# Two-layer hybrid decoder on one core: the first K group of the first turn, 256 rows, becomes two of 128 rows, with two blocks held in PSUM and a shorter filler

## The reference

```python
mod = jax.nn.silu(c) @ w_ada + b_ada                 # w_ada: 2048 x 6144
shift, scale, gate = jnp.split(mod, 3, axis=-1)
h = _rmsnorm(x, norm_pre) * (1.0 + scale[:, None, :]) + shift[:, None, :]
z = h @ w_in                                         # w_in: 2048 x 14336
gb, gcin, u, g_c, q, k, v, g_r = jnp.split(z, offs, axis=-1)
y_conv = gb * _causal_short_conv(gcin * u, conv_w) * jax.nn.silu(g_c)
ret = _head_groupnorm(_retention_chunkwise(rope(q), rope(k) * RET_DK ** -0.5, v), gn_gain)
y_ret = ret * jax.nn.silu(g_r)
o = jnp.concatenate([y_conv, y_ret], axis=-1) @ w_out
x = x + gate[:, None, :] * _rmsnorm(o, norm_post)
```

## Time and profile before

| what | value |
|---|---|
| median of 3 runs | 1704.76 us (1704.67 to 1704.78) |
| the profiled execution, its own time | 1705.27 us |
| its span, first to last instruction | 1703.5 us |
| PE busy | 1675.5 us (98%) |
| DVE busy | 1168.8 us (69%) |
| ACT busy | 733.5 us (43%) |
| DMA | 429.25 MB, mean 252 GB/s |

### The profile page before, as it was taken

One profiled execution on the slowest core, in us unless ns is written; L12 is line 12 of the kernel. 1 busy time (PEld: TensorE's weight loads), 2 busy tenths in 40 slices (PEclk: granted clock), 3 DMA queues, 4 the chain that ended last, 5 costly groups with the idle time before them and its releaser, 6 DMA issues.

```text
span 1703.5 us, 19027 instructions
## 1 busy us (share of the span) xinstructions
PE 1675.5 (98%) x7707; PEld 1371.7 (81%) x7707; DVE 1168.8 (69%) x1325; ACT 733.5 (43%) x817; POOL 52.2 (3%) x94
## 2 busy tenths in 40 slices
PE   5999999999999999999999999999999999999998
PEld 4677788888888888888878888888888888888886
DVE  2578768788678778788886455555645555578777
ACT  4454444534444444344464434344344444444442
POOL 4000000000000000000000000000000000000000
PEclk9999999999999999999999999999999999999999
DMA  9999765897798789888865675557556756678884
GB/s 340 383 373 346 229 213 179 290 303 275 242 310 282 251 301 305 307 281 286 292 199 198 198 219 189 186 197 222 180 185 204 222 185 188 209 261 301 286 288 178
DMA packets 233655, 429.25 MB, mean 252 GB/s; under 512 B 8664, under 2 KB 50024, under 8 KB 232800
## 3 DMA queue, kind: packets, MB, share of 16 engines
q1 hardware_dynamic: 225888, 408.97, 70.3%
q10 hardware_dynamic: 7680, 19.07, 4.2%
HBM read 417.57 MB, written 2.10 MB: 246 GB/s over the span
## 4 chain that ended last, share of the span: by engine, by line
PE 97%; DVE 1%; DMA 1%; SPq 0%; issue 0%; ACT 0%; POOL 0%; DVEq 0%; ACTq 0%
PE Z L1398 31%; PE Z L1400 30%; PE Z L1399 30%; PE A L1437 1%; DMA front_last_stage<-in_w_ada 1%; PE A L1486 1%; PE B L1486 0%; SPq L601 0%; PE A L1450 0%; PE A L1579 0%; PE B L1593 0%; PE B L1591 0%; PE B L1592 0%; PE Z L1445 0%; DVE xt L1029 0%; PE A L1580 0%
## 5 line engine op out<-in xcount | busy, mean ns | idle before, releaser
L649 ACT CAST w_hi<-stage 128x1024 fp32r<-128x1024 f32 x574 | 602.5, 1052 | 921.4 <-PE Z L1400 840.0
L885 DVE TENSOR_TENSOR w_lo<-stage,w_hi 128x1024 fp32r<-128x1024 f32 x574 | 696.6, 1222 | 434.5 <-ACT w_hi L649 430.4
L1398 PE MATMUL Z<-w_hi,H 128*128 128x512 f32 x1784 | 702.8, 394 | 0.6 <-DVE part L1135 0.5
L1400 PE MATMUL Z<-w_hi,H 128*128 128x512 f32 x1784 | 695.2, 390 | 0.0
L1399 PE MATMUL Z<-w_lo,H 128*128 128x512 f32 x1784 | 694.7, 389 | 0.0
L1398 PEld LDWEIGHTS Z<-w_hi,H 128*128 128x128 f32 x1784 | 335.0, 188 | 77.9 <-issue 8.4
L1400 PEld LDWEIGHTS Z<-w_hi,H 128*128 128x128 f32 x1784 | 334.9, 188 | 70.6
L1399 PEld LDWEIGHTS Z<-w_lo,H 128*128 128x128 f32 x1784 | 335.2, 188 | 67.7
L906 DVE SCALAR_TENSOR_TENSOR acc<-stage,c_silu,acc 128x512 f32<-128x512 f32 x240 | 180.2, 751 | 6.8
L1398 PE MATMUL Z<-w_hi,YC 128*128 128x512 f32 x256 | 100.2, 391 | 0.0
L1398 PE MATMUL Z<-w_hi,YR 128*128 128x512 f32 x256 | 100.0, 391 | 0.0
(11 more groups left out here) (178 smaller groups left out, 742.7 us busy)
## 6 DMA issues: line engine op xcount, KB each, us to landing
stage<-in_w_in SPq DMA_DIRECT2D x186, 1024.0 KB, 5.2
stage<-in_w_ada SPq DMA_DIRECT2D x64, 1024.0 KB, 5.3
stage<-in_w_out SPq DMA_DIRECT2D x64, 1024.0 KB, 5.3
stage<-in_w_in SPq DMA_DIRECT2D x74, 512.0 KB, 4.8
front_stage<-in_w_ada SPq DMA_DIRECT2D x24, 1024.0 KB, 10.8
front_last_stage<-in_w_ada SPq DMA_DIRECT2D x8, 1024.0 KB, 13.2
behind<-R ACTq DMA_DIRECT2D x14, 448.0 KB, 3.5
taps<-in_conv_w ACTq DMA_DIRECT2D x18, 256.0 KB, 6.4
```

The lines of the kernel that those rows point to most:

```text
L649: N.copy(w_bufs(n, h)[0], stage[:, slot_of(n), 2 * h:2 * h + 2, :]).then_inc(s_hi, 1)
L885: V.tensor_tensor(lo, stage[:, slot_of(n), 2 * h:2 * h + 2, :], hi.bitcast(F32), ALU.subtract)\
L1398: T.matmul(z[:, i, :], hh, wh, start=ch.first and a == 0, stop=False)
L1400: ins = T.matmul(z[:, i, :], hl, wh, start=False, stop=stop)
```

## The change

The first group is split: `FRONT_GROUPS` now begins with two groups of one tile (128 rows) and has six groups. Chunks 0 to 6 are the new group 0, 7 to 13 the new group 1, 14 to 20 the new group 2 (tiles 2 and 3, which were group 1), the early chunks 21 to 23, and everything from there on stands 7 places later. The blocks GG and GB of group 0 stay in their accumulators, and group 1 begins with these two and adds to them; the other five blocks are added on DVE. A piece of w_ada of the first two groups is 16 times 128 rows of 128 columns, where it was 8 times 128 rows of 256 columns (both 1 MiB). The filler is 5 products instead of 8. All tables of the front are new.

```diff
-FRONT_GROUPS = ((0, 2), (2, 2), (4, 4), (8, 4), (12, 4))
+FRONT_GROUPS = ((0, 1), (1, 1), (2, 2), (4, 4), (8, 4), (12, 4))
-EARLY, EARLY_AFTER = (QK, VV, GR), 1
+EARLY, EARLY_AFTER = (QK, VV, GR), 2
+HELD = (GG, GB)
...
-        for b in range(BLOCKS):
-            table.append(Chunk(False, 0, 0, b, g, q, True, True, k0, tiles // 2))
+        every = HELD + tuple(range(HELD[0])) if g == 1 else range(BLOCKS)
+        for at, b in enumerate(every):
+            table.append(Chunk(False, 0, 0, b, g, q, g != 1 or b not in HELD, g != 0 or b not in HELD, k0, tiles, at))
             q += 1
...
-FRONT_LOAD = {2: 2, 4: 2, 7: 2, 9: 2, 11: 2, 14: 2, 16: 2, 18: 2, 21: 2, 22: 2, 24: 2, 25: 2, 28: 2, 29: 2}
+FRONT_LOAD = {1: 1, 2: 1, 4: 1, 5: 1, 6: 1, 7: 1, 12: 2, 14: 2, 18: 2, 21: 2, 23: 2, 25: 2, 28: 2, 29: 2, 31: 2, 32: 2, 35: 2, 36: 2}
...
-FRONT_USE = {1: ((2, 0), (2, 1)), 3: ((3, 0), (3, 1)), 7: ((4, 0), (4, 1)), 9: ((4, 2), (4, 3)),
+FRONT_USE = {1: ((2, 0),), 2: ((3, 0),), 8: ((4, 0), (4, 1)), 10: ((5, 0), (5, 1)), 14: ((6, 0), (6, 1)), 16: ((6, 2), (6, 3)),
...
-FRONT_ROW = {2: 2, 4: 3, 10: 4, 15: 5, 20: 6, 21: 7, 27: 8, 28: 9}
+FRONT_ROW = {2: 2, 3: 3, 9: 4, 11: 5, 17: 6, 22: 7, 27: 8, 28: 9, 34: 10, 35: 11}
...
-FRONT_MOD = {3: (2,), 5: (3,), 11: (4,), 16: (5,), 22: (6, 7), 29: (8, 9)}
+FRONT_MOD = {3: (2,), 4: (3,), 10: (4,), 12: (5,), 18: (6,), 23: (7,), 29: (8, 9), 36: (10, 11)}
-FRONT_H = {6: 1, 23: 3, 30: 4}
-FRONT_H_AMID = {17: 2}
+FRONT_H = {5: 1, 13: 2, 30: 4, 37: 5}
+FRONT_H_AMID = {24: 3}
...
-                if 0 <= n - SPILL < FRONT and CH[n - SPILL].g == 0:
+                if 0 <= n - SPILL < FRONT and copied(n - SPILL):
...
-            bridge(Z[0][:, 0, :], 8)
+            bridge(Z[0][:, 0, :], 5)
```

More of the change, by code:

```diff
@@ L55, with halves @@
 PRM = 272
-FRONT_GROUPS = ((0, 2), (2, 2), (4, 4), (8, 4), (12, 4))
+FRONT_GROUPS = ((0, 1), (1, 1), (2, 2), (4, 4), (8, 4), (12, 4))
 LAST_GROUP = len(FRONT_GROUPS) - 1
-EARLY, EARLY_AFTER = (QK, VV, GR), 1
-Chunk = namedtuple("Chunk", "out l j b g q first last k0 halves")
+EARLY, EARLY_AFTER = (QK, VV, GR), 2
+HELD = (GG, GB)
+Chunk = namedtuple("Chunk", "out l j b g q first last k0 tiles at")
+def halves(c):
+    return -(-c.tiles // 2)
 def chunk_table():
@@ L86, in chunk_table @@
                 for g in range(start, GROUPS):
-                    table.append(Chunk(False, l, j, b, g, q, g == start, g == GROUPS - 1, CK * g, 2))
+                    table.append(Chunk(False, l, j, b, g, q, g == start, g == GROUPS - 1, CK * g, CK, b))
                 q += 1
@@ L99 @@
 FRONT = len(FRONT_GROUPS) * BLOCKS + len(EARLY)
-HALVES = [sum(c.halves for c in CH[:n]) for n in range(len(CH) + 1)]
+HALVES = [sum(halves(c) for c in CH[:n]) for n in range(len(CH) + 1)]
 SPILL = 2
@@ L109 @@
 for c in CH[:FRONT]:
-    if c.g == 0:
+    if not c.last:
+        continue
+    if (c.j, c.b) not in PART_NO:
         PART_NO[c.j, c.b] = len(PART_NO) + 1
@@ L466, in taken, with added, copied @@
             return z_free(block_no(t, b))
+        def added(n):
+            return CH[n].j == 0 and (CH[n].g, CH[n].b) in FIN_NO
+        def copied(n):
+            return CH[n].last and not added(n)
         def fin(b):
@@ L673, in h_full @@
             def h_full(l, k0, tiles):
-                for k in range(k0, k0 + tiles, 2):
-                    h_unit(l, k // 4, k % 4 // 2, None)
+                for g, half in halves_of(k0, tiles):
+                    h_unit(l, g, half, None)
             def x_scaled(g):
@@ L1091, in front_split @@
                 k0, tiles = FRONT_GROUPS[g]
-                for k in range(k0, k0 + tiles, 2):
-                    h_split(0, k // 4, k % 4 // 2)
+                for g_, half in halves_of(k0, tiles):
+                    h_split(0, g_, half)
             V.memset(c_cols[:, :, :], 0.0).then_inc(s_zeros, 1)
@@ L1116, in _ @@
             low(0, 0)
[L1117 removed]
+            front_split(0)
             ada_seen = 0
@@ L1376, in z_wait @@
                 was = CH[ch.q - 2]
-                if ch.q - 2 < FRONT and was.g == 0:
+                if ch.q - 2 < FRONT and copied(ch.q - 2):
                     pe.wait_ge(s_part, PART_NO[was.j, was.b])
@@ L1512, in _ @@
                     z_wait(n)
[L1513 to L1516, removed]
+                    for h in range(halves(ch)):
+                        if not ch.out and ch.at == 0 and ch.j == 0:
+                            g, half = halves_of(ch.k0, ch.tiles)[h]
+                            pe.wait_ge(s_h, UNIT[ch.l, g, half, None] + 1)
                         if ch.out and ch.j == 0 and h == 0:
```

63 lines of the change are left out of this document (36 added, 27 removed).

## The result

The changed kernel takes 1716.89 us (median of 4 runs, 1715.84 to 1718.04) against 1704.76 us: slower by 12.1 us, ratio 1.0069 with a 95% interval of 1.0057 to 1.0081. Two of its four runs lie at 1715.8 to 1715.9 and show a mean granted clock of 0.999, two lie at 1717.9 to 1718.0 and show 0.995 and 0.996; the profiled one is of the second kind. Against the runs of the kernel before that give its median, the lower pair alone is 11.1 us slower, so 1.0 of the 12.1 is the clock. The kernel before has two levels as well: beside the experiments most of its runs lie at 1704.5 to 1705.3, and 2 of 13, 5 of 19 and 3 of 9 at 1706.1 to 1706.4. The changed kernel's profiled span is 1716.1 us, 12.6 longer than before.

A forecast was written before the change was run, and what follows sets the result against it. PE was taken as the bound, with the front's load of 60 MiB close behind. Chunk 14 8.0 us late plus 0.6 at chunk 15 made 8.6 us, from the median 1704.76 to 1713.4; range 1708 to 1718.5.

The forecast's parts named there:

- case A: The front as worked out, all terms summed: slower by 6.5 to 11 us, 1711.3 to 1715.8; chance 0.60.
- case C: Load up to chunk 8: a packet costs a fixed time whatever its bytes, 1716 to 1723 us; chance 0.12.
- (1): Start of the products: less w_ada ahead and a shorter filler bring the first product 5 to 7.5 us earlier.
- (2): Load up to chunk 8: 512-byte packets add 2.4 us; chunk 8 starts at 45.4 against 45.12, head start gone.
- Case B: Load and DVE: 512-byte packets cost no more than 1 KiB ones, DVE freer; 1708.3 to 1711 us; chance 0.14.
- (3): Chunk 8 to 14: PE still has four pieces, columns and two sums to do, putting it 4.3 us behind.
- (4): Ahead of chunks 12, 13 and 14: new waits for DVE of 0.8, 1.1 and 1.8 us, together 3.7.
- (5): Chunk 15: its load lands at 63 to 64 and its w_lo comes late; 0.6 us added.
- The clock: Stretch behind the starved one: a granted clock of 0.50 there can lose up to 1.7 us.

The follow-up runs named there:

- packets_1k: Changed kernel, but the four w_ada pieces of the first two groups are read as 8 times 128 rows of 256 columns (1 KiB packets); 1716.54 us, ratio 1.0063.
- half_load_after: Changed kernel with only half the rows of each w_ada piece of its first three groups loaded and multiplied twice, 4 MiB less; ratio 1.0019 to the kernel before.
- early_uses: Changed kernel with pieces (4, 0) to (5, 1) multiplied behind chunks 5 to 8, and their rows, sums and split two chunks earlier; 1714.50 us.
- the spread loads: Pieces (6, 0) to (6, 3) issued singly behind chunks 12 to 15, on top of the changed kernel with earlier-multiplied pieces; 1711.66 us.
- adds_small: Changed kernel with the five DVE adds of group 1 cut to 8 columns instead of 1024, waits and order kept; 1716.61 us, ratio 1.0072.
- spread_adds_small: Changed kernel with pieces multiplied earlier and group 3 loads issued singly, plus the five DVE adds of group 1 cut to 8 columns; 1711.20 us.
- loads_as_before: Changed kernel with the pieces of group 3 issued behind chunks 14, 16, 18 and 21 instead of 12, 14, 18 and 21; 1715.71 us.
- half_load_before: Kernel before with only half the rows of each w_ada piece of its first two groups loaded and multiplied twice, 4 MiB less; 1701.94 us, ratio 0.9981.
- filler8: Changed kernel with 8 filler products again instead of 5; 1717.07 us, ratio 1.0070.
- no_held: Changed kernel without held accumulators: GG and GB of group 0 copied too, group 1 in usual order with seven DVE adds; 1715.99 us.
- filler_starved: Changed kernel with 4 more filler products behind each of chunks 4, 5, 6 and 7, where PE waits for data; 1716.93 us, ratio 1.0069.

## Why the prediction came out as it did

The direction, the place and the mechanism are those of case A; the size is larger: 12.1 us instead of 8.6, within the range and above A's own, which ended at 11 (1715.8). By the number alone 1716.9 falls to case C, whose cause packets_1k rules out.

**(1) and (2), the start and the load.** Chunk 0 came at 22.55 (22 to 24.5 foreseen), the head start was gone by chunk 8 at 45.54 (45.4 foreseen), in four waits ahead of chunks 5 to 8, of 3.5 to 3.7 us from start to start, about the 3.7 that the load of 1.25 MiB was reckoned at. half_load_after shows that the load is the cause. Within (2) the price of the 512-byte packets was taken too high, 2.4 us where packets_1k shows 1.3 at chunk 8 (1.4 and 2.2 between runs of like clock); that chunk 8 was hit within 0.2 us all the same is partly luck: another part of that sum was up to 1 us too low, and I can't say which. Case B's free packets and case C's packets of fixed time are both out. The Trainium skill (DMA: Bandwidth & Descriptors, section Specifications) gives 512 B as the least transfer for line rate; that does not hold in this trace: 307 GB/s with such packets, 349 without.

**(3), the pieces behind chunks 8 and 10.** Worked out at 4.0 us more between chunk 8 and chunk 14. early_uses, which moves them into the starved stretch, gives 2.4 us by the median; together with the spread loads it is 5.2.

**(4), the waits ahead of chunks 12, 13 and 14.** They came out at 0.7, 1.3 and 1.7 us from start to start, in sum the 3.7 that was worked out, but the step failed in its cause: it has an add of 1.13 us in the path of each of the three waits. The adds are worth 1.0 us by the profiles (adds_small) and 0.5 by the medians of spread_adds_small. Three things end at about the same time there: DVE's adds, the late load of chunk 13, and the chain over the sums, ACT's h and the split. loads_as_before has chunk 13's load early, still waits 0.80 and 1.66 us ahead of chunks 13 and 14, and takes as long from chunk 9 to chunk 14 as the changed kernel (13.2 and 13.1 us), so that load alone is worth nothing; adds_small has small adds and waits for the load and the chain. By this most of the 3.7 us belongs to the chain, which was in the reckoning of chunk 14 and which no run takes away alone. I had the load done by then.

**(5), chunk 15.** The step that was mis-sized: 0.6 us foreseen, 2.0 measured (70.95 - 64.31 = 6.6, where chunk 7 to chunk 8 took 4.7). I let the load rest from 47 to about 49 us; it rested from 44 to 52. With four slots for chunks of 0.25 MiB the whole lookahead of that ring is 1 MiB, and the other ring was full of pieces that PE had not yet used. Chunk 15's weights came at 67.5, where 63 to 64 was reckoned.

**The clock.** Left out of the sum and put into A's upper part at up to 1.7 us. In the profiled run it fell at 36 us and chunk 8 and what follows took 5.6 us where 3.6 was reckoned. Profiles with the clock at 1.00 there took 3.86, so 1.8 us of this is the clock, nearly half of the difference between forecast and profile. The runs show both cases, 1715.9 and 1717.9.

Added up for the profiled execution, against the kernel before: 0.4 at chunk 8, 4.0 for the pieces, columns and sums, 3.7 of waits, 1.8 of clock, 2.0 at chunk 15, and 0.7 that is mostly the chunks themselves: 1.37 us was reckoned for each, and those that start behind other work took 1.5 to 1.6 until the next thing began (chunks 9 to 11: 1.46, 1.55 and 1.51). That is 12.6 in all. What stays open is the last 5.5 us between half_load_after and half_load_before: its profile puts 4.5 of them into the waits ahead of chunks 12 to 15, but no experiment took them all away.

## What to carry to other kernels

Before starting the first products earlier, ask what the stage behind them is bound by: here a filler shortened by three products in the old kernel brought chunk 0 2.4 us forward and was worth nothing, since the load had less than 1 us in hand some 45 us later. A split into smaller groups halves the work that hides each load and, with rings counted in slots, shrinks the bytes in flight as well; look for the moment at which both rings wait for the engine that they feed. And where several chains end together, a reckoning can hit the size of a wait with the wrong cause, and taking away one of them shows only the little by which it ends last: here 1.0 us of 3.7 for the adds, nothing for the load.

## What the runs showed of the hardware

- Loads in packets of 512 bytes ran at 307 GB/s (14 to 24 us of the changed kernel, with some chunks of 2 KiB packets among them), those of 1 KiB at 349 (the same window of packets_1k), those of 2 KiB at 387.
- The granted clock of PE fell to 0.50, 1.2 of 2.4 GHz, in some executions of one and the same kernel and, by their times and mean clocks, not in others, for 2.0 us of the total. A fall that was over by 46 us, while PE still waited for data, cost nothing (3.86 us from chunk 8 to chunk 9 in adds_small and filler8, as in no_held without a fall).
- In the profile of filler_starved the stretch at the low clock began at 69.7 us, just behind waits of 1.54 and 1.92 us, with products of 0.23 us from start to start between them; it lasted until 73.1, and there the products took 0.43 us from start to start.
